# Up stages whose norm factor is applied behind the products, in a two-layer kernel on one core

## The reference

```
# layer 1
x = x + gate * rms_norm(mixed @ w_o, post_g)            # "o1": a norm of the product, then the residual
h = rms_norm(x, ffn_pre_g) * (1 + scale) + shift        # "the second norm" of the layer
u = causal_conv_3_taps(h @ w_up) + b_conv               # 1024 -> 2 * 2816, per feature
x = x + gate * rms_norm((silu(gt) * val) @ w_down, ffn_post_g)
# layer 2
x = x + gate_a * ((g_a * o_a + g_b * o_b) @ w_o)        # "o2": no norm of the product
h = rms_norm(x, ffn_norm) * (1 + scale_f) + shift_f
u = causal_conv_3_taps(h @ w_up) + b_conv
x = x + gate_f * ((silu(gt) * val) @ w_down)
```

## Time and profile before

| | |
|---|---|
| median of 3 runs | 1058.37 us (1056.8 to 1060.44) |
| span of the profiled execution, first to last instruction | 1056.5 us |
| TensorE busy | 1025.1 us (97%) |
| GpSimd, ScalarE, VectorE busy | 689.8, 634.4, 556.2 us |
| mean granted TensorE clock | 0.997 of full |

### The profile page before, as it was taken

How to read it: one execution, slowest core, us unless ns; L and a number is a source line. 1 busy time by engine, 2 the same in 40 slices (tenths; PEclk the granted TensorE clock), 3 DMA queues, 4 the chain that set the end, 5 groups by cost and what they waited for, 6 DMA issues and landing times.

```text
span 1056.5 us, 23232 instructions
## 1 busy us (share of the span) xinstructions
PE 1025.1 (97%) x8537; PEld 966.4 (91%) x8537; DVE 556.2 (53%) x1165; ACT 634.4 (60%) x1133; POOL 689.8 (65%) x306
## 2 busy tenths in 40 slices
PE   7999999999999989999999899999989999999998
PEld 5999999988799979999999799998667699999998
DVE  2577625579874435565522542296566735444400
ACT  4555764477774576666645656744566557666642
POOL 2598899811269855988799287790031075988795
PEclk9999999999999999999999999999999999999999
DMA  9988888655547863777687289865201043665563
GB/s 380 383 306 282 273 307 298 235 191 187 174 146 259 282 236 105 273 235 248 204 279 268 80 283 360 330 239 191 99 21 60 1 140 122 217 193 189 168 217 111
DMA packets 62616, 226.43 MB, mean 214 GB/s; under 512 B 6960, under 2 KB 8272, under 8 KB 61264
## 3 DMA queue, kind: packets, MB, share of 16 engines
q1 hardware_dynamic: 61344, 221.23, 60.5%
q10 hardware_dynamic: 1200, 4.23, 1.4%
HBM read 224.35 MB, written 1.08 MB: 213 GB/s over the span
## 4 chain that ended last, share of the span: by engine, by line
PE 75%; issue 9%; POOL 9%; DVE 3%; ACT 3%; DMA 1%; POOLq 0%; ACTq 0%; DVEq 0%; SPq 0%
PE psL L553 68%; POOL WL L505 8%; PE psO L553 3%; PE psS L553 2%; PE psL L1092 1%; DMA ring<-wts 1%; ACT psL L1685 0%; ACT WH L1155 0%; ACT R L1273 0%; PE psS L1036 0%; ACT L1146 0%; DVE sm L2288 0%; PE psS L1063 0%; PE psS L966 0%; DVE CT L2052 0%
## 5 line engine op out<-in xcount | busy, mean ns | idle before, releaser
L505 POOL TENSOR_TENSOR WL<-ring,WH 128x1024 fp32r<-128x1024 f32 (+1 forms) x282 | 670.4, 2399 | 239.8 <-ACT WH L1155 186.7
L553 PE MATMUL psL<-HR,WH 128*128 128x256 f32 (+1 forms) x3096 | 513.5, 278 | 1.8 <-DVE HR L1796 0.9
L553 PEld LDWEIGHTS psL<-HR,WH 128*128 128x128 f32 (+1 forms) x3096 | 452.6, 187 | 7.5 <-issue 4.8
L553 PE MATMUL psL<-HR,WL 128*128 128x256 f32 x1536 | 396.2, 276 | 0.0
L1155 ACT ACTIVATE WH<-ring 128x1024 fp32r<-128x1024 f32 (+1 forms) x210 | 216.5, 1042 | 107.8 <-PE psL L553 71.9
L553 PEld LDWEIGHTS psL<-HR,WL 128*128 128x128 f32 x1536 | 275.2, 188 | 0.0
L553 PE MATMUL psL<-RR,WH 128*128 128x256 f32 x1356 | 205.2, 277 | 2.4 <-DVE RR L1981 1.2
L553 PEld LDWEIGHTS psL<-RR,WH 128*128 128x128 f32 x1356 | 185.5, 187 | 3.8 <-issue 2.8
L553 PE MATMUL psL<-RR,WL 128*128 128x256 f32 x672 | 145.0, 277 | 0.3 <-POOL WL L505 0.3
L2080 DVE SCALAR_TENSOR_TENSOR CT<-psL,par,CT 128x254 f32<-128x254 f32 (+1 forms) x176 | 80.9, 480 | 107.1 <-ACT CT L1463 102.0
L1454 ACT ACTIVATE WH<-ring 128x1024 fp32r<-128x1024 f32 (+1 forms) x88 | 92.9, 1058 | 71.4 <-PE psL L553 68.0
(11 more groups left out here) (274 smaller groups left out, 1122.8 us busy)
## 6 DMA issues: line engine op xcount, KB each, us to landing
ring<-wts SPq DMA_DIRECT2D x285, 512.0 KB, 4.2
adaring<-ada_w SPq DMA_DIRECT2D x80, 512.0 KB, 4.8
R<-ada_w SPq DMA_DIRECT2D x8, 1024.0 KB, 16.2
ring<-wts SPq DMA_DIRECT2D x16, 384.0 KB, 3.8
R<-cum_dram ACTq DMA_DIRECT2D x8, 512.0 KB, 4.1
R<-wts SPq DMA_DIRECT2D x8, 512.0 KB, 6.4
ring<-wts SPq DMA_DIRECT2D x8, 288.0 KB, 2.8
adaring<-wts SPq DMA_DIRECT2D x4, 512.0 KB, 5.2
```

The source lines that it names most:

```text
L505: nc.gpsimd.tensor_tensor(WL[:, k, 0:n], ring[:, k, 0:n], WH[:, k, 0:n].bitcast(F32), SUB).then_inc(lo_done, 1)
L553: return nc.tensor.matmul(out, lhsT, rhs, start=start, stop=stop)
```

## The change

Four things are changed.

1. **Factor behind the products.** The up products no longer wait for the norm. Their operand is now `gain * X` without the root (GH and GL, the high and low part). Each operand tile is two columns wider (T2 = 258), and the two leading columns hold minus the shift. `shift_pads` and `low_pads` write them once. After a unit VectorE makes a per-feature bias from column 0 of the bank and the sum of the taps (`tap_sums`, BCOL), and multiplies the 256 other columns in the bank by the root (`scale`). ScalarE and VectorE then go on as before, but read shifted columns of the bank.
2. **Order.** In front of up1 X is updated in pieces, its tiles go to the first three units at once (`up_tiles`), and the 8 blocks of the sum of squares stand between them. In front of up2 the operand tiles are made while o2 runs (`gained` in psO, `up2_low`), and the sum stands after the first four tiles.
3. **One table set.** `roots_table` names the set that holds both Ln and Exp at the start of the o1, down1 and o2 stages. `preload` goes.
4. **Root and part in PSUM.** `root_in_bank` leaves the root in its psS bank, and the residual updates write root * part to a psL bank instead of CT.

The core of the diff:

```diff
+T2 = T + 2
+        def gained(m):
+            return psO[:, m % 2, 0:T]
+            def up_tiles(name, base, tiles):
+                u0, q0 = PLAN.at[name][1], PLAN.q(name)
+                for k in tiles:
+                    pe.wait_ge(h_ready, base + k + 1)
+                    for c in range(3):
...
+                        last = triple(psL[:, (u0 + c) % 4, 0:T2], WH[:, s, k * P:(k + 1) * P], WL[:, s, k * P:(k + 1) * P],
+                                      g_hi(k), g_lo(k), k == 0, k == 7)
             pe.wait_ge(rs_ready, 6)
-            fill(u0, 5)
-            stat("stat_ffn1", sq_at, 8, base=13)
-            fill(u0, 6)
-            pe.wait_ge(rs_ready, 7)
-            fill(u0, 4)
-            linear8("up1", 0, 44, h_hi, h_lo, from_count(h_ready, 8), 3, 5, True)
+            fill(u0, 14)
+            pe.wait_ge(pad_lo, 1)
+            up_tiles("up1", 8, (0, 1))
+            out = scratch("stat_ffn1")
+            for part in range(3):
+                for k in (2 * part, 2 * part + 1):
+                    stat_block(out, k, 8, sq_at, 13)
+                if part < 2:
+                    up_tiles("up1", 8, (2 * part + 2, 2 * part + 3))
+            for k in (6, 7):
+                stat_block(out, k, 8, sq_at, 13)
+            up_tiles("up1", 8, (6, 7))
+            linear8("up1", 0, 44, g_hi, g_lo, None, 3, 5, True, T2)
...
-            fill(u0, 7)
+            pe.wait_ge(pad_lo, 2)
+            up_tiles("up2", 24, range(4))
             stat_of_sums("stat_ffn2", 3)
-            fill(u0, 7)
-            pe.wait_ge(rs_ready, 12)
-            fill(u0, 4)
-            linear8("up2", 0, 44, h_hi, h_lo, from_count(h_ready, 24), 3, 5, True)
+            up_tiles("up2", 24, range(4, 8))
+            linear8("up2", 0, 44, g_hi, g_lo, None, 3, 5, True, T2)
...
-            def preload():
-                st.link(A(sm[:, 94:95], eps_col[:, :], ACT.Ln))
+            def roots_table():
+                nc.scalar.preload_act_table_set("natural_log_exp_and_others")
+            def root_in_bank(name):
+                act.wait_ge(s_done, SCRATCH[name] + 1)
+                st.link(A(RS[:, 0, :], sbank(name)[:, 0:T], ACT.Ln, scale=1.0 / D, bias=eps_col[:, :]))
+                A(sbank(name)[:, 0:T], RS[:, 0, :], ACT.Exp, scale=-0.5).then_inc(rs_ready, 1)
...
+            def up_operand(j):
+                act.wait_ge(x_ready, j + 1)
+                A(GH[:, j, 2:T2], X[:, j, :], ACT.Identity, scale=lead[:, 16 + j:17 + j]).then_inc(hh_ready, 1)
...
+                        act.wait_ge(f_scaled, 4 * (base + j) + 2 * b + 2 + it * 4)
+                        A(CT[:, 2 * slot + b, :], psL[:, u % 4, 2:T2], ACT.Identity,
...
+            def up_low(j):
+                dve.wait_ge(hh_ready, 8 + j + 1)
+                V.scalar_tensor_tensor(GL[:, j, 2:T2], X[:, j, :], lead[:, 16 + j:17 + j], GH[:, j, 2:T2].bitcast(F32),
+                                       MUL, SUB).then_inc(h_ready, 1)
...
+                def scale(j, slot, b, it):
+                    u = u0 + 2 * j + b
+                    bank = psL[:, u % 4, :]
+                    dve.wait_ge(lin_done, u + 1 + it * 2)
+                    V.tensor_scalar(BCOL[:, 2 * slot + b:2 * slot + b + 1], bank[:, 0:1], NWS[:, bass.ds(b * KF + j + it, 1)],
+                                    par[:, bass.ds(b0 + b * KF + j + it, 1)], MUL, ADD).then_inc(f_scaled, 1)
+                    V.tensor_tensor(bank[:, 2:T2], bank[:, 2:T2], rs, MUL).then_inc(f_scaled, 1)
...
                             if back == 1:
+                                if j > 0 or b == 0:
+                                    scale(j, slot, b, it)
+                                if j == 0 and b == 0:
+                                    scale(j, slot, 1, it)
+                                if fill and b == 0:
+                                    fill()
                                 dve.wait_ge(f_begun, 2 * base + 2 * j + b + 1 + it * 2)
```

More of the change, by code:

```diff
@@ L603, in thin_products, with late_unit @@
                     mm(psL[0:32, u % 4, T:2 * T], weights, rhs, True, True)
-            def late_unit(u, q, nchunks, hi, lo, operand=None, thin=False):
+            def late_unit(u, q, nchunks, hi, lo, operand=None, thin=False, width=T):
                 bank_wait(u)
-                out = psL[:, u % 4, 0:T]
+                out = psL[:, u % 4, 0:width]
                 for c in range(nchunks):
@@ L643, in together, with linear8 @@
                             last.then_inc(lin_done, 1)
-            def linear8(name, first, count, hi, lo, operand=None, joint=0, late=0, thin=False):
+            def linear8(name, first, count, hi, lo, operand=None, joint=0, late=0, thin=False, width=T):
                 q0, u0 = PLAN.q(name) + first, PLAN.at[name][1] + first
-                if joint:
+                if joint and operand:
                     together(u0, q0, joint, hi, lo, operand)
@@ L2061, in _ @@
             dve.wait_ge(evac_done, 8)
-            add_normed(MIX, RS[:, 0, :], 0)
-            dve.wait_ge(x_ready, 8)
-            dve.wait_ge(rs_ready, 7)
-            make_h(mod[:, 24:32], lead[:, 16:24], RS[:, 1, :], 8)
-            def ffn(name, wname, base, between):
-                u0 = PLAN.at[name][1]
-                w0 = PAR[wname][0]
-                def conv(j, slot, it=0, uses=0):
+            root = sbank("stat_o1")[:, 0:T]
+            part = psL[:, (PLAN.at["up1"][1] + 3) % 4, :].rearrange("p (a b) -> p a b", b=T)
@@ new lines, in _ @@
+            scaled_part(0, 1, 0)
+            add_part(0, 1, 0)
+            scaled_part(1, 1, 1)
+            add_part(1, 1, 1)
+            up_low(0)
+            up_low(1)
+            scaled_part(2, 2, 0)
+            add_part(2, 2, 0)
+            scaled_part(4, 2, 0)
+            up_low(2)
+            up_low(3)
+            add_part(4, 2, 0)
+            scaled_part(6, 2, 0)
+            up_low(4)
+            up_low(5)
+            add_part(6, 2, 0)
+            dve.sem_inc(s_free[SCRATCH["stat_o1"] % 2], 1)
@@ L2410, in add_gated @@
                     dve.sem_inc(x_ready, 1)
-                    if sq_base is not None and m >= 1:
-                        add_squares(m - 1, sq_base)
+                    if sq_base is not None:
+                        if m >= 2:
+                            dve.wait_ge(h_ready, 24 + m - 1)
+                        V.tensor_scalar(gained(m), X[:, m, :], lead[:, 8 + m:9 + m], None, MUL).then_inc(t_ready, 1)
+                        if m == 1:
+                            low_pads(mod[:, 24:32], 2)
+                        if m >= 1:
+                            add_squares(m - 1, sq_base)
+                            up2_low(m - 1)
                 if sq_base is not None:
                     add_squares(7, sq_base)
+                    up2_low(7)
+            tap_sums("fconv_w_2")
             add_gated("o2", mod[:, 16:24], 38)
             dve.wait_ge(rs_ready, 12)
-            make_h(mod[:, 24:32], lead[:, 8:16], RS[:, 0, :], 24)
-            ffn("up2", "fconv_w_2", KF, None)
+            ffn("up2", "fconv_w_2", "fconv_b_2", RS[:, 0, :], KF, None)
             add_gated("down2", mod[:, 40:48])
```

147 lines of the change are left out of this document (98 added, 49 removed).

## The result

The changed kernel takes 1063.92 us (median of 6 runs, 1062.47 to 1066.44), the kernel before 1059.1 (6 runs, 1056.8 to 1060.44). The ratio is 1.0053, 95% interval 1.0038 to 1.0069: about 5.6 us slower by this ratio, where 11 us faster was forecast. The profiled execution has a span of 1064.6 us and was the longest of the six; the one of the kernel before has 1056.5.

The account below looks back on a forecast made before the run. TensorE was taken as the bound, with 75% of the chain of waits. Terms 6.0 + 3.3 + 5.4 - 1.9 - 2.6 = 10.2 us off the 1056.5 us span gave 1046.3, median 1048; range 1044 to 1054 us.

Parts of the forecast that it names:

- A: From o1 to up1's fourth unit: an earlier start, 6.0 us gained.
- B: From down1 to tok2: root loads gone, shorter pauses and a partly kept clock, 3.3 us gained.
- C: From o2 to up2's fourth unit: operand made while o2 runs, 5.4 us gained.
- the second rival: In front of up1: GpSimd's split holds up the first low part, up to 2.4 us, 1050; chance 8%.
- D: Up1 and up2: two columns more per product, time going with columns, 1.9 us lost.
- products of more than 256 columns run at another rate: Rival on the widened products: a tenth more per product is 24 us, 1072; chance 3%.
- My sign for a slow VectorE: In up1: units taking over 2.8 us would mean VectorE paces the stage.
- E: Scaling in the bank in the up stages, VectorE's lag felt at the start of down1: 2.6 us lost.
- The hops: In up1's units: hop to ScalarE 0.14, its start 0.55, hop back 0.14 us.
- The small bias instruction: Ahead of each unit's scaling on VectorE: 0.16 us long, about 0.08 until the next.
- the bank's slack of 2.6 us: Inside up1: bank free at about 466.8, needed at 469.4, so TensorE wouldn't feel VectorE's lag there.
- B's residual term: At down1: the first residual instruction reads only one tensor in SBUF, counted as 0.1 us.

Follow-up runs that it names:

- before_258: Kernel before with 258 instead of 256 columns in up1's and up2's products after the first three units, tiles still 256 apart; 1076.03 us, ratio 1.0150.
- before_254: Kernel before with 254 columns per product from the fourth unit of up1 and up2, starts and distances as before; 1072.11 us, one run.
- before_240: Kernel before with 240 columns per product from the fourth unit of up1 and up2, starts as before; 1060.12 us, one run.
- before_start8: Kernel before with each 256-column operand starting 8 bytes further from the fourth unit of up1 and up2; 1076.95 us, one run.
- before_start64: Kernel before with each 256-column operand starting 64 bytes further from the fourth unit of up1 and up2; 1077.5 us, one run.
- after_256: Changed kernel with 256-column products from the ninth unit of up1 and up2, six thin products ahead, tiles still 258 apart; 1060.78 us, ratio 1.0021.
- after_stride264: Changed kernel with tiles 264 instead of 258 columns apart, products still 258 wide; 1058.76 us, ratio 1.0001.
- after_thin_down: Changed kernel with six thin products (32 columns of weights) ahead of the first unit of down1 and of down2; 1061.37 us, ratio 1.0032.
- after_plain_256: Changed kernel without the two shift columns: tiles 256 columns apart, products 256 wide; 1056.85 us, ratio 0.9986.
- plain_no_scale: after_plain_256 with VectorE's scaling in the bank covering 2 columns instead of 254; 1045.95 us, ratio 0.9881.

## Why the prediction was wrong

- **A, B, C held**, within half a microsecond each (5.7 plus 0.7, 3.6, 4.9). No load stands at a root, and with 1.28 us a load the sums gave 6.0 and 3.3. The drain of the Trainium skill (ScalarE: Activation LUTs, What ACT_TABLE_LOAD costs), by which A and B would have gained some 4 us more, doesn't show. The low part of tile 0 started at 387.55, 0.3 us after GpSimd's split ended (384.92 + 2.35): the second rival missed by as little as I had written. The clock stayed up between down1 and tok2, but in the attention, which the change doesn't touch, TensorE ran at half clock for 6.8 us instead of the 3.4 us before.
- **D failed.** This is the step that turned the sign. The term was "If time goes with columns it is 0.1133 x 2 / 256 = 0.0009 us each, 1.9 us in all". It was 0.0077 us each, 15.2 us in all, and before_258 shows the loss with nothing else changed. I had this as a rival ("products of more than 256 columns run at another rate", 1072 us) and gave it 3%, on the ground that no row had such a product. No row is no evidence against. The rival's mechanism was near, but it isn't a step at 256 columns: a start 8 or 64 bytes later costs 5 to 6% too, and with 254 columns a product took longer than with 256. Why TensorE takes longer for these stays open. And the trace before had a sign that the time of a product isn't fixed: the same product took 8.58 / 72 = 0.119 us in up1's first three units and 0.1133 behind them, 0.115 in up2's. I used both numbers and never asked why one product has two times. My sign for a slow VectorE misled as well. Units in up1 took 24 x 0.1210 = 2.90 us, over the 2.8 that I had written, and VectorE didn't pace the stage.
- **The down stages** were in no term. Their products of 256 columns ran at 0.1178 us in the profile of the changed kernel and in some experiments (before_254, before_240, before_start8, before_start64), at 0.1133 in others (before_258, after_256, after_stride264, after_thin_down). So the 4.8 us in the table belong to this profiled execution, and it isn't shown that the change causes them. What decides between the two rates stays open.
- **E was mis-sized and mis-placed, and it was hidden.** VectorE's cycle was 5.64 and 5.82 us, not 5.47 and 5.71. The hops were right: ScalarE's turn leaves VectorE idle for 0.85 us (438.58), and I had 0.83. The small bias instruction was not. It takes 0.27 us and 0.19 until the next one starts (437.12 to 437.31), and from a row of 128x2 I had 0.16 and 0.08. I looked at the bank's slack of 2.6 us inside the stage. The weights' split ran out first, behind ScalarE's queue. In the changed kernel the hole at down1 was 0.5 us, since D's slow products cover the rest. With D gone the scaling costs 11 (after_plain_256 against plain_no_scale), in up1 about half by waits and half by the slower rate: 96 products from the hole at 436.05 on ran at 0.118. A hole doesn't always bring that rate, since after the one of 1.52 us at down1 TensorE ran fast (311 products from 540 to 575 us).
- **B's residual term**, 0.1 us for PSUM, held only as part of the whole. Without it the instruction takes 2.08 us at o1 and 2.14 at down1, and the gain of the tables is mostly lost at these two places.

Taken together: plain_no_scale, with A, B and C and neither D nor E, takes 1045.95 us. The forecast without D and E is 1048.2 - 1.9 - 2.6 = 1043.7. So the gains were there. D took them and hid E.

## What to carry to other kernels

A tuned matmul loop may sit on a shape and start of its operand at which TensorE is fast. Measure the new width and start in the old kernel, each alone, before anything is built on them. When a bound seems to move, look first whether the engine is busy throughout. If it is, count its instructions in a window and look at the steps between their starts: equal longer steps point at the instruction itself, single long ones at waits that the busy row hides. When an instruction is made to wait, list what is queued behind it on its engine, to the end of the chain. And a stall that is removed may move the next instruction onto a port that another engine holds.

## What the runs showed of the hardware

- fp32r products of 128 x 128 weights in the up stages, time each by the window's count: 256 columns starting on multiples of 1024 bytes of their buffer 0.113 us, 240 columns 0.112, 254 columns 0.118, 258 columns 0.1215, 256 columns starting 8 or 64 bytes later 0.120 and 0.119, 256 and 258 columns on multiples of 1032 bytes 0.120 and 0.121, 258 on multiples of 1056 bytes 0.120; all at 2.4 GHz granted.
- The same 256-column product has a second rate of 0.1178 us, which lasted over whole down stages in some profiled executions. No run shows what brings it.
- In down1, 256-column products whose buffer lies 256 or 512 bytes further ran at the fast rate (before_258, after_stride264: 311 products in 35 us, 312 in the kernel before).
- A VectorE instruction with both inputs and its output in SBUF took 2.08 us beside a GpSimd split, 0.69 with one input and the output in PSUM.
- In up1 of after_plain_256 TensorE's busy row shows 99.49 of 100 us, and still 37 products fewer than in plain_no_scale (845 against 882).
